# The opening of a two-layer transformer kernel: adaLN pieces, low parts and parameters placed anew

## The reference

```python
cond = silu(c)
mod = cond @ w_ada[l] + b_ada[l]            # 1024 x 9216: shift, scale and gate of three blocks
h = rms_norm(x, norm_g[l, 0]) * (1 + sc1) + sh1
x = x + 0.5 * g1 * swiglu(h, w_ff_in[l, 0], w_ff_out[l, 0])
h = rms_norm(x, norm_g[l, 1]) * (1 + sc2) + sh2
x = x + g2 * token_mix(h, ...)              # attention, RG-LRU and gated linear attention, merged by gates
h = rms_norm(x, norm_g[l, 2]) * (1 + sc3) + sh3
x = x + 0.5 * g3 * swiglu(h, w_ff_in[l, 1], w_ff_out[l, 1])
```

## Time and profile before

| | |
|---|---|
| median of three runs | 1542.37 us |
| the profiled execution | 1542.24 us, its span 1540.5 us |
| TensorE busy | 1507.8 us, 98% of the span |
| VectorE busy | 1140.4 us, 74% |
| ScalarE busy | 800.3 us, 52% |
| GpSimd busy | 25.2 us, 2% |
| HBM read | 330.23 MB, 215 GB/s over the span |
| first two of 40 slices, PE busy in tenths | 6 and 9, all others 9 but the last |
| first two of 40 slices, granted clock | 0.8 and 0.8, all others 0.9 or more |

### The profile page before, as it was taken

One profiled execution on the slowest core, in us unless ns is written; L12 is line 12 of the kernel. 1 busy time (PEld: TensorE's weight loads), 2 busy tenths in 40 slices (PEclk: granted clock), 3 DMA queues, 4 the chain that ended last, 5 costly groups with the idle time before them and its releaser, 6 DMA issues.

```text
span 1540.5 us, 29168 instructions
## 1 busy us (share of the span) xinstructions
PE 1507.8 (98%) x12530; PEld 1462.0 (95%) x12530; DVE 1140.4 (74%) x1547; ACT 800.3 (52%) x970; POOL 25.2 (2%) x29
## 2 busy tenths in 40 slices
PE   6999999999999999999999999999999999999998
PEld 5999998999999999999999999999999899999998
DVE  6697777898546998776877768769865589977454
ACT  4344346888546446433464444677855544464342
POOL 0000000000100000000000000000001000000000
PEclk8899999999999999999999999999999999999999
DMA  9989864554456995888658785555454589676551
GB/s 322 321 264 275 273 189 145 151 171 138 138 164 227 308 312 192 270 273 291 204 193 292 260 295 168 152 164 151 140 163 147 174 303 340 221 252 202 168 194 54
DMA packets 287073, 333.52 MB, mean 216 GB/s; under 512 B 13084, under 2 KB 241344, under 8 KB 286944
## 3 DMA queue, kind: packets, MB, share of 16 engines
q1 hardware_dynamic: 279184, 327.40, 65.0%
q10 hardware_dynamic: 7760, 4.26, 1.2%
HBM read 330.23 MB, written 1.38 MB: 215 GB/s over the span
## 4 chain that ended last, share of the span: by engine, by line
PE 79%; DVE 11%; ACT 7%; issue 2%; DMA 1%; ACTq 0%; SPq 0%; DVEq 0%
PE ps L501 66%; DVE w_lo L1484 4%; PE ps L874 3%; ACT w_hi L1005 2%; DVE scratch L1380 2%; DVE hf L1541 1%; DVE h_lo L1546 1%; PE ps L789 1%; PE ps L585 1%; PE ps L545 1%; DVE xT L1561 1%; ACT L1018 1%; ACT xm L1031 1%; PE ps L735 1%; PE ps L836 1%
## 5 line engine op out<-in xcount | busy, mean ns | idle before, releaser
L501 PE MATMUL ps<-h_hi,w_hi 128*128 128x256 f32 x2320 | 653.4, 282 | 1.0 <-DVE w_lo L1484 1.0
L501 PE MATMUL ps<-h_lo,w_hi 128*128 128x256 f32 x2320 | 643.7, 277 | 0.0
L501 PE MATMUL ps<-h_hi,w_lo 128*128 128x256 f32 x2320 | 641.8, 277 | 0.0
L1484 DVE TENSOR_TENSOR w_lo<-raw,w_hi 128x2048 fp32r<-128x2048 f32 x238 | 543.5, 2286 | 114.7 <-ACT w_hi L1005 114.7
L1005 ACT ACTIVATE w_hi<-raw 128x2048 fp32r<-128x2048 f32 x237 | 452.6, 1912 | 202.8 <-PE ps L501 198.1
L501 PEld LDWEIGHTS ps<-h_hi,w_hi 128*128 128x128 f32 x2320 | 434.3, 187 | 9.0 <-issue 7.1
L501 PEld LDWEIGHTS ps<-h_lo,w_hi 128*128 128x128 f32 x2320 | 437.9, 189 | 0.5 <-issue 0.5
L501 PEld LDWEIGHTS ps<-h_hi,w_lo 128*128 128x128 f32 x2320 | 434.2, 187 | 0.0
L501 PE MATMUL ps<-xm,w_hi 128*128 128x256 f32 x1408 | 251.0, 281 | 0.0
L501 PEld LDWEIGHTS ps<-xm,w_hi 128*128 128x128 f32 x1408 | 215.1, 189 | 0.0
L501 PE MATMUL ps<-xm,w_lo 128*128 128x256 f32 x704 | 197.0, 280 | 0.0
(11 more groups left out here) (276 smaller groups left out, 1685.8 us busy)
## 6 DMA issues: line engine op xcount, KB each, us to landing
raw<-in_w_ff_in_dram SPq DMA_DIRECT2D x176, 512.0 KB, 4.8
eyr<-in_w_ada_dram SPq DMA_DIRECT2D x144, 512.0 KB, 7.1
raw<-in_w_in_dram SPq DMA_DIRECT2D x100, 512.0 KB, 4.7
raw<-in_w_ff_out_dram SPq DMA_DIRECT2D x88, 512.0 KB, 4.8
raw<-in_w_gate_dram SPq DMA_DIRECT2D x48, 512.0 KB, 4.6
raw<-in_w_branch_dram SPq DMA_DIRECT2D x48, 512.0 KB, 4.5
raw<-in_w_out_dram SPq DMA_DIRECT2D x16, 512.0 KB, 5.8
rgw<-in_rg_w_dram ACTq DMA_DIRECT2D x16, 128.0 KB, 2.4
```

The source lines that it names most:

```text
L501: last = mm(outs, a, b[:, cc, :], start=clear and cc == 0 and q == 0, stop=cc == n - 1 and q == 2, skip_group_check=True)
L1484: tt(w_lo[:, p % SPLIT, :], raw[:, p % RAW, :], w_hi[:, p % SPLIT, :].bitcast(F32), ALU.subtract).then_inc(lo_ready, 1)
```

## The change

- No adaLN piece is multiplied directly: ADA_DIRECT is empty, and VectorE weighs piece 5 too.
- SP loads slab 1 right behind slab 0, and pieces 4 to 7 behind it.
- GpSimd makes the low parts of slabs 0 and 1.
- VectorE multiplies xT by rstd into hf ahead (rooted), two banks before piece 3 and two behind it. ACT applies scale and shift together for h_hi, VectorE scales hf in place and subtracts.
- ACT makes both high parts before the first stage's pieces.
- Parameters are loaded under two semaphores, one for each layer, and turned and copied by layer: layer 0's before block 0, layer 1's and the bias table behind block 1; ACT copies the latter behind the first stage.
- stay_busy has 8, 10 and 8 products in place of 6, none and 3.

```diff
-ADA_DIRECT = (5,)
+ADA_DIRECT = ()
-PARAM_LOADS = 12 * DEPTH + 2
+PARAM_LOADS = 12
@@ sync
             load(0, ffi_v[:, 0, 0, :, FF:FF + 256])
-            for a in (4, 5):
-                ada(a)
             load(1, ffi_v[:, 0, 0, :, 0:256])
-            for a in (6, 7):
+            for a in range(4, ADA_START):
                 ada(a)
@@ gpsimd
+            for p in range(2):
+                pool.wait_ge(hi_ready, p + 1)
+                if p:
+                    pool.wait_ge(lo_ready, p)
+                pool.tensor_tensor(w_lo[:, p, :], raw[:, p, :], w_hi[:, p, :].bitcast(F32), ALU.subtract).then_inc(lo_ready, 1)
@@ tensor
-            pe.wait_ge(small_loaded, 16 * PARAM_LOADS)
-            for a in range(2):
-                for l in range(DEPTH):
-                    k = 2 * l + a
-                    last = nc.tensor.transpose(ps[:, 3, k * 96:k * 96 + 96], prow[:, l, a, :], ident[0:96, 0:96])
-            last.then_inc(turned, 1)
-            mm(ps[0:HEADS, 5, 16:16 + NREL], tabl, bkt, start=True, stop=True).then_inc(turned, 1)
+            def parameters(l):
+                for a in range(2):
+                    last = nc.tensor.transpose(ps[:, 3 - l, a * 96:a * 96 + 96], prow[:, l, a, :], ident[0:96, 0:96])
+                last.then_inc(turned, 1)
+            pe.wait_ge(first_loaded, 16 * PARAM_LOADS)
+            parameters(0)
             ada(0)
             ada(1)
-            stay_busy(0, 6)
+            pe.wait_ge(small_loaded, 16 * (PARAM_LOADS + 2))
+            parameters(1)
+            mm(ps[0:HEADS, 5, 16:16 + NREL], tabl, bkt, start=True, stop=True).then_inc(turned, 1)
+            stay_busy(0, 8)
...
-                        pe.wait_ge(par_ready, 2)
                         pe.wait_ge(rstd_ready, 1)
                         stage(gate_in[0], 4, *STAGES[0])
+                        pe.wait_ge(par_ready, 3)
+                        pe.wait_ge(rel_saved, 1)
+                        stage(up_in[0], 5, *STAGES[0])
                         ada(2)
-                        stage(up_in[0], 5, *STAGES[0])
+                        stay_busy(0, 10)
                         for p, bank in ((gate_in[0], 4), (up_in[0], 5)):
                             stage(p, bank, *STAGES[1])
                         ada(3)
-                        stay_busy(0, 3)
+                        stay_busy(0, 8)
@@ scalar
-            f(par[:, :, :].rearrange("p l n -> p (l n)"), ps[:, 3, 0:DEPTH * NPAR], ACT.Copy).then_inc(par_ready, 1)
-            act.wait_ge(loaded[0], 32)
-            f(w_hi[:, 0, :], raw[:, 0, :], ACT.Copy).then_inc(hi_ready, 1)
...
+            f(par[:, 0, :], ps[:, 3, 0:NPAR], ACT.Copy).then_inc(par_ready, 1)
+            act.preload_act_table_set("silu_and_others")
...
+                def opening_pieces(s):
+                    act.wait_ge(ma_opened, s + 1)
+                    for cc in range(*STAGES[s]):
+                        act.wait_ge(hf_ready, cc + 1)
+                        f(h_hi[:, cc, :], hf[:, cc, :], ACT.Identity, scale=ma[:, cc:cc + 1],
+                          bias=ms[:, cc:cc + 1]).then_inc(hhi_ready, 1)
...
+                        hi(gate_in[0])
                         hi(up_in[0])
-                        pieces(q, chunks=STAGES[1])
+                        opening_pieces(0)
+                        act.wait_ge(turned, 3)
+                        f(par[:, 1, :], ps[:, 2, 0:NPAR], ACT.Copy).then_inc(par_ready, 1)
+                        f(ph[:, 0, :], ps[:, 3, 0:NPAR], ACT.Copy, scale=0.5)
+                        f(ph[:, 1, :], ps[:, 2, 0:NPAR], ACT.Copy, scale=0.5).then_inc(par_ready, 1)
+                        f(brel, ps[0:HEADS, 5, 16:16 + NREL], ACT.Copy).then_inc(rel_saved, 1)
+                        act.wait_ge(rel_saved, 1)
+                        act.dma_start(rel_scratch[:, :, :], brel.unsqueeze(1).broadcast_to((HEADS, 16, NREL))).then_inc(rel_stored, 16)
+                        opening_pieces(1)
                         hi(gate_in[1])
-                        pieces(q, chunks=STAGES[2])
+                        opening_pieces(2)
@@ vector
-            for a in range(4):
+            def rooted(*banks):
+                dve.wait_ge(rstd_ready, 1)
+                for b in banks:
+                    tt(hf[:, 2 * b:2 * b + 2, :], xT[:, 2 * b:2 * b + 2, :], rstd[:, 0:T].unsqueeze(1).broadcast_to((P, 2, T)),
+                       ALU.mult).then_inc(hf_ready, 2)
+            for a in range(3):
                 weigh(a)
+            rooted(0, 1)
+            weigh(3)
             ada(0)
+            rooted(2, 3)
             ada(1)
...
-                    for step in range(first, end + 2):
-                        if step < end:
-                            stt(hf[:, step, :], xT[:, step, :], ma[:, step:step + 1], rstd[:, 0:T], ALU.mult,
-                                ALU.mult).then_inc(hf_ready, 1)
...
+                    for cc in range(first, end):
+                        dve.wait_ge(hhi_ready, cc + 1)
+                        steps.did(ts(hf[:, cc, :], hf[:, cc, :], ma[:, cc:cc + 1], ms[:, cc:cc + 1], ALU.mult, ALU.add))
+                        steps.wait()
+                        tt(h_lo[:, cc, :], hf[:, cc, :], h_hi[:, cc, :].bitcast(F32), ALU.subtract).then_inc(h_ready, 1)
...
-                        lo(gate_in[0])
                         dve.wait_ge(ada_saved, 2)
                         opening_stage(*STAGES[0])
-                        weigh(4)
-                        lo(up_in[0])
-                        weigh(6)
+                        for a in (4, 5, 6):
+                            weigh(a)
                         ada(2)
```

More of the change, by code:

```diff
@@ L216, in build @@
          sq_ready, ss_done, rstd_ready, hf_ready, hhi_ready, h_ready, silu_ready, hid_made, hid_hi_ready, hid_ready,
[L217 removed]
+         consts_ready, bias_masked, fold_ready, ada_folded, ma_ready, mhi_ready, mlo_ready, xhi_ready, xlo_ready, lead_scaled, c_loaded, first_loaded, small_loaded, ma_opened, x_loaded, c_turned, turned, x_turned, par_ready, lam_ready, lam_exp,
          cond_ready, rel_saved, rel_stored, bias_loaded, rgw_loaded, rg_done, wg_loaded, alpha_done, kraw_ready, glr_saved,
@@ L227, in build @@
              "sq_ready ss_done rstd_ready hf_ready hhi_ready h_ready silu_ready hid_made hid_hi_ready hid_ready "
-             "consts_ready bias_masked fold_ready ada_folded ma_ready mhi_ready mlo_ready xhi_ready xlo_ready lead_scaled c_loaded small_loaded x_loaded c_turned turned x_turned par_ready lam_ready lam_exp "
+             "consts_ready bias_masked fold_ready ada_folded ma_ready mhi_ready mlo_ready xhi_ready xlo_ready lead_scaled c_loaded first_loaded small_loaded ma_opened x_loaded c_turned turned x_turned par_ready lam_ready lam_exp "
              "cond_ready rel_saved rel_stored bias_loaded rgw_loaded rg_done wg_loaded alpha_done kraw_ready glr_saved "
@@ L948, in _, with rows, parameters @@
             f(cond[:, :], ps[:, 5, 0:C], ACT.Silu).then_inc(cond_ready, 1)
[L950 to L963, removed]
+            def rows(l, a, r0, src, n, signal):
+                act.dma_start(prow[r0:r0 + n, l, a, :], src.rearrange("(r f) -> r f", f=P)).then_inc(signal, 16)
+            def parameters(l, signal):
+                rows(l, 0, B_ADA, b_ada[l], 72, signal)
+                rows(l, 0, B_NORM, norm_g[l].rearrange("a d -> (a d)"), 24, signal)
+                rows(l, 1, B_CONVW - 96, conv_w[l].rearrange("a d -> (a d)"), 32, signal)
+                rows(l, 1, B_CONVB - 96, conv_b[l], 8, signal)
+                rows(l, 1, B_RGB - 96, rg_b[l].rearrange("a d -> (a d)"), 16, signal)
+                rows(l, 1, B_LAM - 96, rg_lambda[l], 8, signal)
+                rows(l, 1, B_GBG - 96, gla_bg[l], 4, signal)
+                rows(l, 1, B_GNG - 96, gla_norm_g[l], 2, signal)
+                rows(l, 1, B_GATE - 96, b_gate[l], 24, signal)
                 for half in range(2):
-                    act.dma_start(prow[94:96, l, 1, half * HD:(half + 1) * HD], qk_norm_g[l, :, :]).then_inc(small_loaded, 16)
-                act.dma_start(sinks[:, l, :], attn_sinks[l:l + 1, :].broadcast_to((P, HEADS))).then_inc(small_loaded, 16)
-            parameters(0)
+                    act.dma_start(prow[94:96, l, 1, half * HD:(half + 1) * HD], qk_norm_g[l, :, :]).then_inc(signal, 16)
+                act.dma_start(sinks[:, l, :], attn_sinks[l:l + 1, :].broadcast_to((P, HEADS))).then_inc(signal, 16)
+            parameters(0, first_loaded)
             for b in range(4):
@@ L974, in _ @@
                 f(hf[:, 2 * b:2 * b + 2, :], xT[:, 2 * b:2 * b + 2, :], ACT.Square).then_inc(sq_ready, 1)
-            parameters(1)
+            parameters(1, small_loaded)
             act.dma_start(tabl, rel_bias[:, :]).then_inc(small_loaded, 16)
@@ L1038, in norm, with pieces @@
                     rsqrt(rstd[:, 0:T], ps[:, 0, 0:T], D, rstd_ready)
-                def pieces(q, lead_silu=False, chunks=(0, C)):
+                def opening_pieces(s):
[4 more added lines that the diff above has]
```

(16 more changed lines are left out.)

10 lines of the change are left out of this document (2 added, 8 removed).

## The result

The changed kernel takes 1546.48 us (median of ten runs, 1545.5 to 1547.5), the kernel before 1542.13 (ten runs, 1540.5 to 1543.87). The ratio is 1.0025, with a 95% interval of 1.0016 to 1.0034: slower, by 4.35 us between the medians (2.5 to 5.2 us by the interval) where +2.9 was forecast, inside the range (1538.0 to 1548.5) and inside the likeliest case's own range (1543.9 to 1547.7). The profiled execution of the changed kernel took 1547.5 us, span 1545.8; it is the slowest of the ten, so part of the 5.3 us by which its span exceeds the one before is the spread of runs.

What follows compares the result with a forecast made beforehand. TensorE's own products bound the steady part, so the opening's shift is handed on: last stage product at 59.4 instead of 56.5 us, +2.9 on 1542.37 gives 1545.3 us; range 1538.0 to 1548.5.

Steps and rivals of the forecast that it cites:

- likeliest case: Whole kernel: GpSimd and VectorE hold each other up in the opening; +2.9 us, 1545.3 us, own range 1543.9 to 1547.7.
- What bounds the kernel: Steady part: bound by TensorE's own products, so the opening's loss or gain is handed on one for one.
- GpSimd's subtraction: Low parts of slabs 0 and 1: 4.5 us each, between bounds of 1.9 and 9.3.
- rival C: Low parts on GpSimd: each slab takes the upper bound of 9.3 us; +8 to +12, 1552 us; chance 0.05.
- The hold in the other order: Opening: VectorE's two-input modulation of stage 0 stands from 26.9 to 30.6 us, until GpSimd's running subtraction ends.
- A: Opening: the engines don't hold each other up in that order; likeliest -3.2 us, 1539.1; chance 0.32.
- B: Opening: VectorE keeps its turn, GpSimd only gets in between pieces; -1 to +1 us, 1542.4; chance 0.08.
- Pieces in a row: VectorE ahead of block 2's copy: pieces 4, 5, 6 take 8.9 us with gaps, until 47.5 us.
- From stage 1 to the last stage: End of opening: stage 1 begins 48.5 us, piece 7 ends 53.2, fillers 55.8, last stage product 59.4.
- Rival D: Last stages: the fill doesn't hold the clock, both remaining stages at 1.2 GHz; +5.3 us, 1547.6; chance 0.13.
- Piece 5, order of loads, parameters, root: Opening: piece 5 adds 3.11 us on VectorE; no load on the path; root products replace eight multiplications; TensorE free 0.9 later.
- SP's queue: Loads: slab 5 stands behind piece 9's load, 3 us later than before, covered by three slabs (17 us).

Runs made afterwards that it cites:

- the second version above: Changed kernel, both low parts on VectorE, piece 5 direct ahead of the wait for piece 4, fewer fillers, accumulation start flag corrected: 1539.6 us, ratio 0.9980.
- The run with memsets: Changed kernel with GpSimd's two subtractions replaced by memsets of zero, low parts of slabs 0 and 1 left out: 1540.63 us, ratio 0.9993.
- the first experiment: Changed kernel with the low parts of slabs 0 and 1 back on VectorE, the rest as changed: 1542.02 us, ratio 1.0003.

## Why the prediction was right, step by step

- *What bounds the kernel.* Right. The run of products begins 4.43 us later, and the medians differ by 4.35. In the 400 us behind it TensorE is busy for 397.54 us before and 397.52 after. The agreement is not as fine as it looks: from the beginning of this run to the end the twelve profiled executions need 1485.3 to 1486.4 us, and 1487.8 and 1488.7 in two of them (piece 5 direct again, and the second version above), so a shift is handed on with the spread of runs on top.
- *GpSimd's subtraction.* 4.5 us were taken; it is 4.78 and 4.68, of which a part may be waiting for VectorE. The upper bound of the two reads (9.3) and rival C are out.
- *The hold in the other order.* The step without a row, and the one on which the sign hung. Forecast: modulation from 26.9 to 30.6, stage 0's h_lo done at 38.6. Measured: 27.25 to 30.90, and 38.67. GpSimd got in between VectorE's small steps as said. For the second hold the prediction had the subtraction (two inputs) stand still and the scaling pass; it was the scaling that was held, which comes to the same time, since the subtraction follows it. Rivals A and B fall. The run with memsets comes nearest to A's price: 5.85 us, with a hold of 1.1 still in it, where 1545.3 - 1539.1 = 6.2 had been put between them.
- *Pieces in a row.* Forecast 47.5, measured 47.72 for the copy.
- *From stage 1 to the last stage.* This is the mis-sized term, and with it the +2.9. Forecast: block 3's first h_hi at 55.1, fillers to 55.8, slab 2's low part at about 59, last product at 59.4. Measured: h_hi at 56.2, fillers to 57.69, slab 2's low part at 60.05, last product at 61.09. Of the 1.7 us, 0.5 had come up by the end of piece 7 (53.70 for 53.2): 0.2 at block 2's copy, the rest in stage 1, where a scaling takes 0.41 and not 0.33 and the first waits 0.67 for ACT; another 0.6 lies in the steps from block 3 to h_hi. The remaining 0.6 came up in the last stage, where the fillers and the first products had the low level from 55.3 to 58.6. What the low clock cost in all can be estimated: behind a low part that ends at 60.05 the run could have begun at 60.2, by the 0.15 us of the first experiment, so it cost 0.9 us in this execution, against the 0.7 that the forecast had in it (59.4 in place of 58.7). Rival D held for half of its stretch; no run took its price by itself.
- *Piece 5, order of loads, parameters, root.* Forecast as no net loss beyond VectorE's 3.1 us. The first experiment says it as a sum: all of the change but GpSimd's part is worth -0.1 us (1.0003, 0.9994 to 1.0012). Parameters and root were not tried one by one, so which of them gains what piece 5 costs stays open. The traces say where it is gained: with both low parts on VectorE, block 2's copy comes 1.4 us later than before, counted from slab 0's high part (42.63 - 22.87 against 42.26 - 23.88), and the run of products follows it in 12.5 us instead of 14.4, at a granted clock of 1.00. The prediction was wrong to say that the root's products take the place of eight multiplications: a chunk of stage 0 takes VectorE 0.8 us with them, as it did before, so their 2.6 us come on top. They fit in ahead of block 1's copy, which still waits 0.68 us for TensorE. Its reading that the clock fell after block 2 is a little off as well: it fell within it, at the third of its four columns.
- *SP's queue.* Slab 5 was issued at 46.17, 1.8 us later than before (3 were forecast), and slab 6 after 12.6 us of waiting at 60.08; the DMA queues stood still from 56 to 61. TensorE waited for none of it, as said.

## What to carry to other kernels

In this kernel, work moved to GpSimd was not taken off VectorE, because it read SBUF while VectorE ran operations with two SBUF inputs or scalings within SBUF: 4.5 us of VectorE's subtractions became 7.1 us of holds (3.65 - 0.15 and 4.02 - 0.41), and they lay in front of the smallest steps of the path. Look for them as long durations of tiny operations. The idle engine of this opening was TensorE, between two stages: the version with the same 1 MiB piece done there, ahead of a wait and not behind it, was 3 us faster than the kernel before. Behind the wait, in the changed kernel, it gained nothing over weighing. Fillers are not free either: at the low clock eight of them take about 3 us, and they stood on the path.

## What the runs showed that had not been expected

A memset by GpSimd, which reads nothing, held VectorE's scaling of 256 elements (1.48 us instead of 0.41), and at the same time let additions with two inputs pass (0.16 us). The prediction had held only operations with two inputs for endangered; the second hold of the changed kernel (4.02 us) fell on a scaling. TensorE's clock came back from a gap of 3.25 us at the low level, and from one of 2.8 us once at the high and once at the low one. In the kernel before with GpSimd's part alone the level stayed at 0.51 for 17 us, of which TensorE was busy for 12.7; the same direct products ran at the high level in the changed kernel with piece 5 direct. Which of the two levels a stretch gets was not settled.
